# One core, two transformer blocks: first weight tile in halves, norm row one tile later in two feed-forwards, another order in the last norm

## The reference, cut to what matters

```python
def rms_norm(x, w):
    x32 = x.astype(jnp.float32)
    y = x32 * lax.rsqrt(jnp.mean(x32 * x32, axis=-1, keepdims=True) + EPS)
    return y.astype(x.dtype) * w

def swiglu(h, w_in, w_out):
    gate, up = jnp.split(h @ w_in, 2, axis=-1)
    return (jax.nn.silu(gate) * up) @ w_out
...
x = x + 0.5 * swiglu(rms_norm(x, norm_ffn1_w[l]), ffn1_w_in[l], ffn1_w_out[l])
```

## Time and profile before

| | |
|---|---|
| median of 3 runs | 1942.42 us (1942.16 to 1943.93) |
| the profiled execution | 1942.74 us |
| its span in the profile | 1940.4 us |
| TensorE busy | 1879.5 us (97%) |
| VectorE busy | 1287.8 us (66%) |
| ScalarE busy | 972.7 us (50%) |
| GpSimd busy | 152.1 us (8%) |
| mean granted clock of TensorE | 0.987 |

### The profile page before, as it was taken

The page is one execution under the profiler, slowest core; times in us unless marked ns, Lnnn a source line. Parts: engine busy times, 40 slices in busy tenths (PEclk is TensorE's granted clock), DMA queues, the critical chain, the costliest instruction groups (busy, mean ns, idle before and its releaser), DMA issues.

```text
span 1940.4 us, 32368 instructions
## 1 busy us (share of the span) xinstructions
PE 1879.5 (97%) x13202; PEld 1731.9 (89%) x13202; DVE 1287.8 (66%) x1454; ACT 972.7 (50%) x1322; POOL 152.1 (8%) x169
## 2 busy tenths in 40 slices
PE   6999999999999998999999999999999989999997
PEld 5999999899999997999999899989999859999997
DVE  6676687776566665766785766676668675456665
ACT  5454555565354444444654544554455464445443
POOL 2020100131010003000120100010000001010001
PEclk9999999999999998999999999999999889999998
DMA  6655354434435554555443455545545303435553
GB/s 240 229 184 186 140 185 152 142 131 154 154 149 193 177 193 147 187 187 186 160 174 131 174 193 178 187 179 176 193 173 201 131 23 141 164 112 214 181 187 108
DMA packets 45699, 324.77 MB, mean 167 GB/s; under 512 B 5165, under 2 KB 5301, under 8 KB 6688
## 3 DMA queue, kind: packets, MB, share of 16 engines
q1 hardware_dynamic: 44352, 316.57, 45.2%
q0 software_dynamic: 1248, 6.77, 1.0%
HBM read 322.26 MB, written 1.06 MB: 167 GB/s over the span
## 4 chain that ended last, share of the span: by engine, by line
PE 71%; DVE 6%; POOL 2%; ACT 1%; issue 1%; POOLq 0%; DVEq 0%; ACTq 0%
PE PS L638 21%; PE PS L545 11%; PE PS L547 11%; PE PS L546 11%; PE PS L641 10%; DVE xT L1991 2%; DVE w_lo L1968 1%; DVE x L2035 1%; PE PS L708 1%; PE PS L726 1%; POOL both L459 1%; PE PS L1258 1%; PE PS L1238 1%; PE PS L1219 1%; DVE mT_lo L1991 0%
## 5 line engine op out<-in xcount | busy, mean ns | idle before, releaser
L1968 DVE TENSOR_TENSOR w_lo<-raw,w_hi 128x2048 fp32r<-128x2048 f32 x298 | 686.4, 2307 | 236.9 <-ACT w_hi L1307 236.6
L638 PE MATMUL PS<-xT,w_hi 128*128 128x512 f32 x2112 | 755.6, 401 | 20.2 <-DVE w_lo L1968 16.4
L1307 ACT ACTIVATE w_hi<-raw 128x2048 fp32r<-128x2048 f32 x299 | 571.0, 1911 | 318.8 <-PE PS L547 300.1
L641 PE MATMUL PS<-xT,w_lo 128*128 128x256 f32 x2112 | 594.4, 281 | 0.0
L638 PEld LDWEIGHTS PS<-xT,w_hi 128*128 128x128 f32 x2112 | 399.2, 189 | 118.9 <-issue 16.3
L641 PEld LDWEIGHTS PS<-xT,w_lo 128*128 128x128 f32 x2112 | 401.1, 190 | 0.2
L545 PE MATMUL PS<-h_hi,w_hi 128*128 128x256 f32 x1280 | 364.2, 285 | 0.0
L546 PE MATMUL PS<-h_lo,w_hi 128*128 128x256 f32 x1280 | 362.1, 283 | 0.0
L547 PE MATMUL PS<-h_hi,w_lo 128*128 128x256 f32 x1280 | 362.0, 283 | 0.0
L545 PEld LDWEIGHTS PS<-h_hi,w_hi 128*128 128x128 f32 x1280 | 245.1, 191 | 4.2 <-DVE h_lo L2115 1.0
L546 PEld LDWEIGHTS PS<-h_lo,w_hi 128*128 128x128 f32 x1280 | 245.2, 192 | 0.2
(11 more groups left out here) (310 smaller groups left out, 2501.1 us busy)
## 6 DMA issues: line engine op xcount, KB each, us to landing
raw<-weights SPq DMA_DIRECT2D x299, 1024.0 KB, 4.8
arena<-mems POOLq DMA_DIRECT2D x5, 1024.0 KB, 6.1
x<-x_in SPq DMA_DIRECT2D x2, 512.0 KB, 4.4
out<-x SPq DMA_DIRECT2D x4, 256.0 KB, 2.5
both<-toep POOLq DMA_DIRECT2D x1, 512.0 KB, 3.9
arena<-toep POOLq DMA_DIRECT2D x1, 512.0 KB, 5.0
con<-consts SPq DMA_DIRECT2D x1, 498.0 KB, 9.5
arena<-dtw SPq DMA_DIRECT2D x1, 256.0 KB, 11.5
```

Source lines behind the costliest of these rows:

```text
L638: pe.matmul(PS[:, bank + part, :], w_hi[:, slot, w:w + P], xT[:, k].rearrange("p a b -> p (a b)"), start=k == 0, stop=False, skip_group_ch ...
L641: last = pe.matmul(PS[:, bank + part, 0:S], w_lo[:, slot, w:w + P], xT_hi[:, k, :], start=False, stop=k == KC - 1, skip_group_check=True)
L1307: act.activation(w_hi[:, slot, :], raw[:, raw_slot, :], ACT.Copy).then_inc(hi_ready, 1)
L1968: dve.tensor_tensor(w_lo[:, slot, :], raw[:, raw_slot, :], w_hi[:, slot, :], ALU.subtract).then_inc(lo_ready, 1)
```

## The change

1. *Start.* The gain columns of the first norm (8 of `col`) are a transfer of their own and the first; then half of x, half of tile 0, the other halves, tiles 1 and 2, and behind them the constants, the other columns and `dtw`. ScalarE and VectorE split tile 0 in two halves, the first between the chunks of x, and TensorE waits for the halves one by one. ScalarE calls Silu on one column at the very start, which moves a table load there. ScalarE's squares come behind the rounding of tile 1. TensorE, ScalarE and VectorE wait for the constants where they need them.
2. *Norm row later in two feed-forwards* (the first, and the one with two norms): the sums come behind tile 1 and the row between the halves of tile 2. VectorE adds tile 0 without the row, then does the rest of tile 3, then the statistic.
3. *Squares by TensorE* in the first stage and the last norm: GpSimd adds chunks 0 to 4, TensorE sums chunks 5, 6 and 7 beside `acc` (`square_sums`).
4. *Last norm.* ScalarE multiplies x by the gain meanwhile; VectorE multiplies pairs of chunks by the row straight out of PSUM.

```diff
-            for m in range(2):
-                sp.dma_start(x[:, 4 * m:4 * m + 4, :], x_in[:, 4 * m:4 * m + 4, :]).then_inc(setup_x[m], 16)
-            sp.dma_start(col[:], cols).then_inc(setup_col, 16)
-            for n in range(RAW):
+            sp.dma_start(col[:, 0:8], cols[:, 0:8]).then_inc(setup_gain, 16)
+            sp.dma_start(x[:, 0:4, :], x_in[:, 0:4, :]).then_inc(setup_x[0], 16)
+            sp.dma_start(raw[:, 0, 0:1024], weights[0][:, 0:1024]).then_inc(first_landed, 16)
+            sp.dma_start(x[:, 4:8, :], x_in[:, 4:8, :]).then_inc(setup_x[1], 16)
+            sp.dma_start(raw[:, 0, 1024:2048], weights[0][:, 1024:2048]).then_inc(landed[0], 16)
+            for n in range(1, RAW):
                 sp.dma_start(raw[:, n, :], weights[n]).then_inc(landed[n], 16)
-                if n == 0:
-                    sp.dma_start(con[:], consts).then_inc(setup, 16)
-                if n == 1:
-                    sp.dma_start(dtw_raw, dtw).then_inc(setup_small, 16)
+            sp.dma_start(con[:], consts).then_inc(setup, 16)
+            sp.dma_start(col[:, 8:NCOLS], cols[:, 8:NCOLS]).then_inc(setup, 16)
+            sp.dma_start(dtw_raw, dtw).then_inc(setup_small, 16)
...
-                sp.wait_ge(scaled, 2 * c + 2)
+                sp.wait_ge(normed, c + 1)
...
-                statistic(rcol, i == DOUBLE)
+                statistic(rcol, i == DOUBLE, 5 if i == 0 or stage == "finalnorm" else KC)
...
+            def square_sums(bank):
+
+                for c in (5, 6, None, 7):
+                    if c is None:
+                        pe.wait_ge(acc_ready, at.stat + 1)
+                    else:
+                        pe.wait_ge(sq_ready, KC * at.stat + c + 1)
+                    v = acc[:, 0, :] if c is None else sq[:, c, :]
+                    for j in range(2):
+                        last = pe.matmul(PS[:, bank, j:j + 1], v[:, j * P:(j + 1) * P], con[:, K_ONES:K_ONES + 1],
+                                         start=c == 5 and j == 0, stop=c == 7, skip_group_check=True)
+                last.then_inc(sum_done, 1)
...
+                            if halves and part == 0 and k % 4 == 0:
+                                pe.wait_ge(lo_ready if k else first_lo, 1)
...
-                paired(n0, n0 % SPL, 4, at.norm - 1)
-                statistic_sums(double)
-                paired(n0 + 1, (n0 + 1) % SPL, 6, None, lambda: statistic_row(double))
-
-                pe.wait_ge(rrow_ready, at.stat)
-                def pair(it, s, mid=None, first=False):
+                paired(n0, n0 % SPL, 4, at.norm - 1, halves=f0 == 0)
+                if deferred:
+                    paired(n0 + 1, (n0 + 1) % SPL, 6)
+                    if f0 == 0:
+                        pe.wait_ge(setup, 32)
+                        square_sums(0)
+                    else:
+                        statistic_sums(double)
+                else:
+                    statistic_sums(double)
+                    paired(n0 + 1, (n0 + 1) % SPL, 6, None, lambda: statistic_row(double))
+                    pe.wait_ge(rrow_ready, at.stat)
...
-                    paired(n, (n0 + 2) % SPL, 4)
+                    paired(n, (n0 + 2) % SPL, 4, None, (lambda: statistic_row(double)) if row_inside else None)
...
                     paired(n + 1, (n0 + 3) % SPL, 6)
+                    if row_inside:
+                        pe.wait_ge(rrow_ready, at.stat)
                     down(n + 2, (n0 + 4) % SPL, s, it * 2 + s, first, False)
 
-                pair(0, 0, first=True)
+                pair(0, 0, first=True, row_inside=deferred)
...
-                    statistic_sums()
-                    statistic_row()
+                    square_sums(4)
+                    statistic_row(bank=5)
...
-                act.wait_ge(setup_col, 16)
+                act.wait_ge(prep, 1)
+                act.activation(small[:, 496:497], minus_half[:, 0:1], ACT.Silu)
+                act.wait_ge(setup_gain, 16)
                 for c in range(KC):
                     if c % 4 == 0:
                         act.wait_ge(setup_x[c // 4], 16)
                     act.activation(xT_hi[:, c, :], x[:, c, :], ACT.Copy, scale=column("ffn0", c)).then_inc(xhi_ready, 1)
-                split(0, 0, 0, 1)
+                    if c == 3:
+                        act.wait_ge(first_landed, 16)
+                        act.activation(w_hi[:, 0, 0:1024], raw[:, 0, 0:1024], ACT.Copy).then_inc(first_hi, 1)
+                act.wait_ge(landed[0], 16)
+                act.activation(w_hi[:, 0, 1024:2048], raw[:, 0, 1024:2048], ACT.Copy).then_inc(hi_ready, 1)
+                split(1, 1, 1, 1)
                 for c in range(KC):
                     square(c, x, 0)
-                for n in range(1, SPL):
-                    split(n, n, n, 1)
+                split(2, 2, 2, 1)
...
+                if double or f0 == 0:
+                    up_low(n0 + 2, 0)
+                    next_split()
+                    statistic_row(rrow, double)
+                    silu(0, 0)
+                else:
+                    statistic_row(rrow)
+                    silu(0, 0)
+                    up_low(n0 + 2, 0)
+                    next_split()
                 hidden_hi(0, 0)
...
-                    statistic_row(rrow)
+                    for c in range(KC):
+                        act.activation(x[:, c, :], x[:, c, :], ACT.Copy, scale=column("fnorm", c)).then_inc(scaled, 1)
...
+                    if c == 3:
+                        dve.wait_ge(first_hi, 1)
+                        dve.tensor_tensor(w_lo[:, 0, 0:1024], raw[:, 0, 0:1024], w_hi[:, 0, 0:1024],
+                                          ALU.subtract).then_inc(first_lo, 1)
+                dve.wait_ge(hi_ready, 1)
+                dve.wait_ge(first_lo, 1)
+                dve.tensor_tensor(w_lo[:, 0, 1024:2048], raw[:, 0, 1024:2048], w_hi[:, 0, 1024:2048],
+                                  ALU.subtract).then_inc(lo_ready, 1)
+                for n in range(1, SPL):
...
+                def gate_sum(p, i):
                     dve.wait_ge(gate_side, f0 + i + 1)
                     dve.tensor_tensor(gate[:, p], gate[:, p], PS[:, 4:6, 0:S], ALU.add).then_inc(gate_taken, 1)
+
+                def scaled_gate(p, i, add=True):
+                    if add:
+                        gate_sum(p, i)
                     dve.wait_ge(gate_taken, f0 + i + 1)
                     dve.tensor_tensor(gate[:, p], gate[:, p], row2, ALU.mult).then_inc(silu_in, 1)
 
-                def product(p, i):
+                def up_sum(p, i):
                     dve.wait_ge(up_side, f0 + i + 1)
                     dve.tensor_tensor(hid[:, p], hid[:, p], PS[:, 6:8, 0:S], ALU.add).then_inc(up_taken, 1)
+
+                def product(p, i, add=True):
+                    if add:
+                        up_sum(p, i)
...
-                statistic(rcol, double)
-                next_split()
-                dve.wait_ge(rrow_ready, at.stat)
-                scaled_gate(0, 0)
-                product(0, 0)
+                if double or f0 == 0:
+                    gate_sum(0, 0)
+                    next_split()
+                    statistic(rcol, double)
+                    up_sum(0, 0)
+                    dve.wait_ge(rrow_ready, at.stat)
+                    scaled_gate(0, 0, False)
+                    product(0, 0, False)
...
-                    statistic(rcol)
-                    dve.wait_ge(rrow_ready, at.stat)
-                    for c in range(KC):
-                        dve.scalar_tensor_tensor(x[:, c, :], x[:, c, :], column("fnorm", c), rrow[:],
-                                                 ALU.mult, ALU.mult).then_inc(scaled, 1)
+                    statistic(rcol, bank=4)
+                    dve.wait_ge(row_done, at.stat)
+                    for c in range(0, KC, 2):
+                        dve.wait_ge(scaled, c + 2)
+                        dve.tensor_tensor(x[:, c:c + 2, :], x[:, c:c + 2, :],
+                                          PS[:, 5, 0:S].unsqueeze(1).broadcast_to([P, 2, S]), ALU.mult).then_inc(normed, 1)
```

46 lines of the change are left out of this document (26 added, 20 removed).

## The result

The changed kernel takes **1929.55 us** (median of 4 runs, 1926.71 to 1930.17) against 1942.52 us for the kernel before beside it (4 runs). The ratio is 0.9928, 95% interval [0.9914, 0.9942]: 13.0 us less, where 11.9 less was forecast (1930.5, range 1927.8 to 1935.0). Timed once more beside later kernels it took 1929.42 (6 runs, ratio 0.9929 [0.9915, 0.9944]).

What follows compares the result with a forecast made beforehand. TensorE, busy nearly all the time, was taken as the bound, so only its standstills and low-clock time could be won. Gains 6.0 + 3.2 + 2.6 = 11.8 us gave 1930.5 us, range 1927.8 to 1935.0.

Steps and rivals of the forecast that it cites:

- Start: First stage, start by halves: first matmul at 9.4 us instead of 16.3, tile 2 ending at 31.8 against 37.8; gain 6.0.
- the landing of the first pieces: Start: halves of x land at 5.1 and 8.6 us, halves of tile 0 at 6.9 and 9.9.
- the wait for GpSimd goes: First stage, sums behind tile 1: TensorE's 0.95 us wait for GpSimd's adds disappears.
- Two norms: Stage with two norms: sums behind tile 1, row inside tile 2; gain 3.2 us, bounds 2.3 to 4.1.
- the place and the price of the clock's fall: Stage with two norms: low clock follows a 3.1 us wait at the row inside tile 2, losing 1.55 us of work.
- if the clock does not fall, it binds: gain 4.1: Stage with two norms: VectorE's chain behind the row, ending 0.9 us early, binds if the clock stays up; gain 4.1 us.
- End: Last norm: statistic 1.75 us sooner, row copy and shorter products 0.4 each; gain 2.6 us, 2.2 if output transfers queue.
- The middle: Feed-forwards between the changed stages: they keep their order and do not depend on when they start; gain 0.
- DMA at the start: Rival, start: x's second half lands at 11, tile 0's at 12, pairs start at 14.6; total 9.3, 1933.1 us; chance 0.12.
- Powers twice as long: Rival, stage with two norms: GpSimd's powers take twice 2.96 us, gain there 0; total 8.6, 1933.8 us; chance 0.10.
- Sums that wait for one another: Rival, last norm: TensorE's sixteen passes queue at the low clock, gain there 0.3; total 9.5, 1932.9 us; chance 0.05.
- Late constants: Rival, first stage: sums wait for constants and last columns behind the weights; slower than before, 1946.5 us; chance 0.02.

Runs made afterwards that it cites:

- a_row_early: The changed kernel with the first stage's sums ahead of tile 1, norm row inside tile 1 and GpSimd adding all eight squares, halves kept: 1935.37 us.
- d_start_old: The changed kernel with the first transfers in their old order and tile 0 whole, later norm row and TensorE's three squares kept: 1934.05 us.

## Why the prediction was right, and where not

- **Start, 6.0 forecast, 5.8 measured; two errors cancelled.** The first matmul came at 10.66, not 9.4. The term at fault is the landing of the first pieces: 5.4, 8.3, 9.6 and 11.1 us (issues at 1.2, 1.7, 2.1 and 2.6 plus 4.2, 6.6, 7.5 and 8.5), where I had 5.1, 6.9, 8.6 and 9.9. I had let the half tile land 1.8 us behind x; it took 2.9, and the windows show 346 and 358 GB/s from 6 to 10 us against the 410 that I had worked out for a later stretch (for which the windows of the kernel before give 384, from 11 to 18 us). Against that the clock rose 5.0 us after the first matmul instead of 5.9, at 15.6 where I had 15.3, and nine of the sixteen pairs ran at the full rate instead of eight; tile 1 starts at 18.74 (forecast 18.4), the sums at 24.29 (24.0), tile 2 at 26.0 (25.9), its end is 32.0 (31.8). That no wait would come ahead of tile 2 or at its row held. That the stage came out 0.2 us off is thus in part luck. Twelve traces of kernels whose start is by halves have the rise 3.4 to 6.2 us after the first matmul, and in the eleven where the sums don't stand before it the weights' tile 1 begins anywhere from 17.7 to 19.5 us. The Trainium skill, "TensorE: Matmul & The Clock Gate", What's actually happening, calls this point run-variable; these traces agree.
- **The halves need the later row and TensorE's squares.** The forecast said that the wait for GpSimd goes, 0.95 us. a_row_early and d_start_old show that the tie is far stronger: without the later row and the three squares the halves lose 1.9 us. The sum by parts had no term for it, and needed none, since both parts were made.
- **Two norms, 3.2 forecast, 3.7 measured, within 2.3 to 4.1.** The first wait was right (1.06 for 1.1; 0.30 for 0.4). The step that failed is the place and the price of the clock's fall. I put it behind the wait at the row and took 1.55 us off the gain. It came ahead of the row, made the wait there 1.22 instead of 3.1, and cost nothing, because VectorE's chain, which I had ending 0.9 us ahead of TensorE, ended last either way. Of my own bounds, "if the clock does not fall, it binds: gain 4.1" was the right mechanism; I should have asked what a fall costs when another chain ends last. Where no fall came, the wait at the row was 2.74 us, near the 3.1.
- **End, 2.6 forecast, 2.2 measured.** Statistic 1.5 to 1.6 for 1.75, copy and products 0.42 + 0.77 for 0.8 (a product took 0.62 and not 0.72), and 0.47 given back by the output transfers, which I had as the lower bound.
- **The middle, 0 forecast, 1.0 measured.** "Nothing in the middle depends on when it starts" was wrong for the clock. Before has a spell of 3.4 us at 1636 to 1640 that the trace of after has not, and there the marks move by 1.3 (9.2 us at the diagonal ahead of it, 10.5 behind); between 1275 and 1464 us they had moved back by 0.3. The parts sum to 11.7, as forecast, and the missing 1.3 us of the median is of this kind. The runs at 1923 us and the one at 1926.71, outside my range, are too: the range had the spread of the first runs of the kernel before (1.8 us) for one of 8.5. Later runs of the kernel before spread as well, 1938.12 to 1944.78.
- **The rivals.** DMA at the start: the first matmul was "10.5 or later", but the second half landed at 11.1 and not 12. Its pairs came at 13.59, between my 12.55 and the rival's 14.6, and the stage lost only 0.2 us, because the clock rose early. The half tile did land 2.9 us behind x, but the next two pieces followed in 1.3 and 1.5 us. The fixed 2 us of the Trainium skill, "DMA: Bandwidth & Descriptors", Anatomy of one DMA, which that section gives for transfers issued by GpSimd (these are SyncE's), is thus not paid in turn here, and the 10 us in all that this reading gave did not come. Powers twice as long: 2.73 us of wait on GpSimd, as before. Sums that wait for one another: 0.58 us for the last four. Late constants: the sums started without a wait.

## To carry over

Edits around one stage should be costed alone as well as together: here one part is worth nothing, the other loses 1.9 us, and the pair gains 5.8. Before a fall of the clock is priced, ask whether TensorE's work or another engine's chain ends the stage; in the shadow of that chain it is free, and once the chain is shortened it costs (0.7 us here). Order the engine that ends last by who waits for its results: moving one statistic and eight products on VectorE was worth 2.3 to 3.0 us.
